# A two-block transformer kernel: residual mix turned by halves in PSUM, attention mask added by VectorE, norm rows fetched earlier, and two expert loads begun by halves

## The reference, cut to what matters

```python
for l in range(2):                       # first block
    mix = conformer_conv(x, ...) if l == 0 else diff_attention(x, ...)
    x = layer_norm(ALPHA * x + mix, ln_mix_g[l], ln_mix_b[l])
    ffn = grouped_moe(x, ...)            # 16 experts of width 512, two for each token
    x = layer_norm(ALPHA * x + ffn, ln_ffn_g[l], ln_ffn_b[l])

h = concat(meta_tokens (16 rows), x)     # second block, 272 rows
xn = rms_norm(h, mix_pre_g)
z, xbc, dt, q, k, v = split(xn @ w_in)
y_ssd = ssd_mixer(z, xbc, dt, ...)       # chunks of 128, the meta rows a chunk of their own
y_sb = rms_norm(stick_breaking_attention(q, k, v), sb_norm_g)
# per head: A[t,s] = sigmoid(z) * prod_{s<j<t}(1 - sigmoid(z)), z = q.k/8, only for s < t
mix = concat([y_ssd, y_sb]) @ w_out
h = h + rms_norm(mix, mix_post_g)
xn = rms_norm(h, ffn_pre_g)
g = causal_dwconv(xn @ w_up[:, :D_FF], conv of 3 taps) # the first token needs two meta rows
f = (gelu(g) * (xn @ w_up[:, D_FF:])) @ w_down
return (h + rms_norm(f, ffn_post_g))[16:]
```

## Time and profile before

| | us |
|---|---|
| median of three runs | 1397.87 (1395.96 to 1400.76) |
| the profiled execution | 1401.46 |
| its span, first to last instruction | 1399.7 |
| PE busy | 1306.0 (93%) |
| DVE busy | 383.9 (27%) |
| ACT busy | 262.6 (19%) |
| POOL busy | 36.0 (3%) |
| moved by DMA | 321.68 MB, mean 230 GB/s |

### The profile page before, as it was taken

How to read it: one execution, slowest core, us unless ns; L and a number is a source line. 1 busy time by engine, 2 the same in 40 slices (tenths; PEclk the granted TensorE clock), 3 DMA queues, 4 the chain that set the end, 5 groups by cost and what they waited for, 6 DMA issues and landing times.

```text
span 1399.7 us, 14987 instructions
## 1 busy us (share of the span) xinstructions
PE 1306.0 (93%) x6166; PEld 815.9 (58%) x6166; DVE 383.9 (27%) x849; ACT 262.6 (19%) x579; POOL 36.0 (3%) x62
## 2 busy tenths in 40 slices
PE   7989899999989998999999799998998979999997
PEld 6754444333437864433433388765775867888743
DVE  0014522111142454312211403455223123222101
ACT  1013311000111343200100321412435012000000
POOL 3110000000000000000000000000000000000000
PEclk9999999999999998999999899899999998999999
DMA  9970899999992063999999923231230162444320
GB/s 307 309 249 2 324 407 428 425 423 429 415 380 86 1 240 147 418 426 424 427 427 427 393 109 121 67 110 43 84 120 1 35 193 73 153 147 161 141 90 30
DMA packets 95087, 321.68 MB, mean 230 GB/s; under 512 B 10099, under 2 KB 47511, under 8 KB 80167
## 3 DMA queue, kind: packets, MB, share of 16 engines
q1 hardware_dynamic: 84368, 301.04, 55.5%
q10 hardware_dynamic: 8662, 12.27, 2.8%
q0 software_dynamic: 1984, 7.34, 1.3%
HBM read 316.30 MB, written 4.34 MB: 229 GB/s over the span
## 4 chain that ended last, share of the span: by engine, by line
PE 87%; DMA 5%; DVE 5%; issue 1%; ACT 1%; DVEq 0%; ACTq 0%; SPq 0%; POOLq 0%
PE psum L255 35%; PE psum L1565 14%; PE psum L1598 7%; PE psum L741 6%; PE psum L2917 5%; DMA ring<-in_moe_w_up 5%; PE psum L1608 4%; PE psum L623 2%; PE psum L909 2%; PE psum L1802 2%; PE psum L531 1%; PE psum L1767 1%; DMA ring<-in_a_w_pw 1%; PE psum L2577 1%; PE psum L1224 1%
## 5 line engine op out<-in xcount | busy, mean ns | idle before, releaser
L255 PE MATMUL psum<-xT,ring 128*128 128x256 f32 (+2 forms) x1792 | 409.7, 390 | 4.6 <-DMA ring<-in_a_w_pw 3.7
L255 PEld LDWEIGHTS psum<-xT,ring 128*128 128x128 f32 x1792 | 344.9, 194 | 65.4 <-issue 10.4
L1565 PE MATMUL psum<-ring,arena 128*64 128x512 f32 x672 | 186.0, 604 | 12.1 <-DMA ring<-in_moe_w_up 6.6
L1565 PEld LDWEIGHTS psum<-ring,arena 128*64 128x64 f32 x672 | 59.8, 139 | 103.1 <-issue 102.8
L1446 DVE TENSOR_TENSOR arena<-psum,arena 64x512 f32<-64x512 f32 x32 | 34.2, 1070 | 215.7 <-ACT arena L1509 215.7
L1598 PE MATMUL psum<-ring,arena 128*64 128x512 f32 x384 | 85.0, 595 | 1.3 <-ACT arena L1526 1.3
L2917 PE MATMUL psum<-ring,arena 128*128 128x512 f32 x176 | 75.7, 592 | 0.0
L1565 PE MATMUL psum<-arena 128*64 128x512 f32 x208 | 70.6, 592 | 0.0
L1509 ACT ACTIVATE arena<-psum 64x512 f32<-64x512 f32 x32 | 18.9, 592 | 269.8 <-PE psum L1565 269.8
L1608 PE MATMUL psum<-arena 128*128 128x512 f32 x128 | 59.5, 605 | 0.0
L2917 PEld LDWEIGHTS psum<-ring,arena 128*128 128x128 f32 x176 | 33.4, 190 | 41.7 <-issue 41.6
(11 more groups left out here) (343 smaller groups left out, 1310.2 us busy)
## 6 DMA issues: line engine op xcount, KB each, us to landing
ring<-in_moe_w_down SPq DMA_DIRECT2D x24, 2048.0 KB, 24.9
ring<-in_moe_w_up SPq DMA_DIRECT2D x22, 2048.0 KB, 20.7
ring<-in_moe_w_gate SPq DMA_DIRECT2D x20, 2048.0 KB, 22.7
ring<-in_w_in SPq DMA_DIRECT2D x11, 2048.0 KB, 22.3
ring<-in_w_up SPq DMA_DIRECT2D x22, 1024.0 KB, 7.7
arena<-in_moe_w_gate SPq DMA_DIRECT2D x6, 2048.0 KB, 26.3
ring<-in_w_down SPq DMA_DIRECT2D x5, 2048.0 KB, 7.8
ring<-in_a_w_pw SPq DMA_DIRECT2D x8, 1024.0 KB, 10.9
```

What stands on the lines that cost most here:

```text
L255: last = nc.tensor.matmul(dst, lhsT, rhs, start=(n == 0), stop=(n == len(pairs) - 1))
L1565: last = pe.matmul(bank(j)[part, :], tokens[:, k, side * SEATS:side * SEATS + SEATS], weights(u + n, k), start=(k == 0), stop=(k == KC - 1))
```

## The change

It has six parts.

1. The rows of the FFN norm of layer 0 are fetched in the conformer stage, behind the last `fetch_shifted`, and those of layer 1 in the attention stage, behind ACT's first four `kq_copy` and a wait for `normed[1]`.
2. The tenth and eleventh unit of each expert layer come by halves (`load_by_halves`): the first halves of both once PE has used slices 0 to 3 of the first `gate_up` (a new semaphore), the second halves when the job is done.
3. One of the 16 q and k products moves from "norm" to chunk 2 of the mixer, ahead of its transposes of xs.
4. The mask is added by DVE (`mask_out`, one operation on both banks), and ACT's `softplus` waits for it. PE's two products go.
5. `project_out`, `mix_post` and `ffn_pre` become `project_out` and `mix_and_turn`. Mix is turned straight into banks 4 to 7 for tiles 1 and 2 (the first half of the width ahead of the last 32 products), the copies to `mix` and the meeting of engines go, ACT and DVE read PSUM, and the tiles go in the order 1, 2, 0.
6. The first four jobs of `ffn` stand as side 1 of c = 0 and 1, then side 0; the first two don't wait until tile 0 of `xT` is copied.

The semaphore of the lambda exponential is replaced by ACT's step semaphore, to make room.

```diff
@@ the loads
+    BY_HALVES = (RING + MORE, RING + MORE + 1)
+        def load_by_halves(layer):
+            first = unit_at[f"moe{layer}"]
+            for half in range(2):
+                if half == 0:
+                    sp.wait_ge(half_used, layer + 1)
+                else:
+                    slot_freed(first + BY_HALVES[0])
+                for u in (first + m for m in BY_HALVES):
+                    kind, _, e = units[u][0]
+                    n = D if kind == "down" else DE
+                    ks = slice(half * 2048 // n, (half + 1) * 2048 // n)
+                    src = a[f"moe_w_{kind}"][layer, e].rearrange("(p k) n -> p k n", p=P)
+                    load(u, src[:, ks, :], slot_k(u, n)[:, ks, :])
...
+                    if (p, side, k) == (0, 0, KC // 2 - 1):
+                        last.then_inc(half_used, 1)
@@ the norm rows
             fetch_shifted(KC - 1)
+            load_norm(1, a["ln_ffn_g"][0], a["ln_ffn_b"][0])
...
+            act.wait_ge(normed[1], 4)
+            load_norm(3, a["ln_ffn_g"][1], a["ln_ffn_b"][1])
             act.preload_act_table_set("natural_log_exp_and_others")
...
     next_norm = {
-        "route0": (1, a["ln_ffn_g"][0], a["ln_ffn_b"][0]), "moe0": (2, a["ln_mix_g"][1], a["ln_mix_b"][1]),
-        "route1": (3, a["ln_ffn_g"][1], a["ln_ffn_b"][1]), "moe1": (4, a["mix_post_g_2"][0]),
+        "moe0": (2, a["ln_mix_g"][1], a["ln_mix_b"][1]), "moe1": (4, a["mix_post_g_2"][0]),
@@ the q and k products
-             ("diag", 2): 2, "norm": 3}
+             ("diag", 2): 2, ("xs", 2): 1, "norm": 2}
@@ the mask
-                first = (BANKS, BANKS + 2, 2)[n % FLIGHT]
-                for side in range(2):
-                    diagonals = psum[:, first + side, :].rearrange("p (a t) -> p a t", a=2)[:, :, 0:P]
-                    last = pe.matmul(diagonals, ident[:, :], not_before[:, :].unsqueeze(1).broadcast_to([P, 2, P]),
-                                     start=False, stop=True, skip_group_check=True)
...
+            def mask_out(n):
+                dve.wait_ge(z_ready, n + 1)
+                first = (BANKS, BANKS + 2, 2)[n % FLIGHT]
+                diagonals = psum[:, first:first + 2, :].rearrange("p s (a t) -> p s a t", a=2)[:, :, :, 0:P]
+                dve.tensor_tensor(diagonals, diagonals, not_before[:, :].unsqueeze(1).unsqueeze(1).broadcast_to([P, 2, 2, P]),
+                                  ALU.add).then_inc(z_masked, 1)
...
+            for n in (2, 3, 4):
+                mask_out(n)
             add_positive(2)
...
                     add_positive(n + 1)
+                if n + 2 < SB_PAIRS:
+                    mask_out(n + 2)
@@ from w_out to the FFN
+            part(0, 0)
+            pe.wait_ge(sb_normed, 1)
+            part(0, 1)
+            part(1, 0)
+            all_read_out(pe, first + 4)
+            for t in (1, 2):
+                turn(0, t)
+            part(1, 1)
+            all_read_out(pe, first + KC)
+            for t in (1, 2):
+                turn(1, t).then_inc(so_summed_mix_turned, 1)
...
+    FFN_ORDER = (1, 2, 0)
...
+            for t in FFN_ORDER:
+                n = TILE_N[t]
+                pe.wait_ge(rms_scaled, base + 4 + count[t])
...
+            for t in FFN_ORDER:
+                mix_squares(t)
+            row_squares(1)
+            row_squares(2)
+            turned_out(1)
+            turned_out(2)
+            row_squares(0)
+            turned_out(0)
...
+            scaled_mix(1)
+            added(1)
+            scaled_mix(2)
+            added(2)
+            scaled_mix(0)
+            scaled_rows(1)
...
+            scaled_rows(2)
+            turned_out(1)
+            turned_out(2)
+            added(0)
+            scaled_rows(0)
+            turned_out(0)
@@ the FFN's jobs
+    UP_ORDER = [(0, 1), (1, 1), (0, 0), (1, 0)] + [(c, side) for c in range(2, FC) for side in range(2)]
+                if j == FJ["up"]:
+                    unit_ready(u)
+                    all_read_out(pe, FJ["ffn_T"] + 4)
+                elif (c, side) == (0, 0):
+                    all_read_out(pe, FJ["up"])
```

More of the change, by code:

```diff
@@ L1741, in turned_heads @@
         return 2 if h < 4 else 3 if h < 6 else 4
+    lam_exp = []
     @stage
@@ L2357, in _ @@
                 n = TILE_N[c]
+                for _ in range(QK_AT.get(("xs", c), 0)):
+                    qk_copy(next(qk_act))
                 if c:
@@ L2841, in _, with part, turn @@
         def _(pe):
[L2843 removed]
+            products(psum[:, BANKS, NEED:L], [(ones[:, :], sqT[:, c, NEED:L]) for c in range(KC)]).then_inc(so_summed_mix_turned, 1)
             w = unit_at["w_out"]
[L2846 to L2847 removed]
+            first, parts = FJ["w_out"], ((w, yT), (w + 1, sbT))
+            def part(half, i):
+                u, lhs = parts[i][0] + 2 * half, parts[i][1]
+                unit_ready(u)
+                for c in range(4 * half, 4 * half + 4):
+                    if i == 0:
+                        take_bank(first + c)
+                    for k in range(KC):
+                        last = pe.matmul(bank(first + c)[:, NEED:L], slot_k(u)[:, k, (c % 4) * P:(c % 4) * P + P],
+                                         lhs[:, k, NEED:L], start=(i == 0 and k == 0), stop=(i == 1 and k == KC - 1))
+                    if i == 1:
+                        last.then_inc(job_done, 1)
+            def turn(half, t):
+                for c in range(4):
+                    last = pe.transpose(psum[:, BANKS + 2 * (t - 1) + half, c * P:c * P + P],
+                                        mixT[:, 4 * half + c, TILE_AT[t]:TILE_AT[t] + P], ident[:, :])
+                return last
+            part(0, 0)
[9 more added lines that the diff above has]
+                turn(1, t).then_inc(so_summed_mix_turned, 1)
+            for half in range(2):
+                j = first + KC + half
+                take_bank(j)
+                for c in range(4):
+                    last = pe.transpose(bank(j)[0:META, c * P:c * P + P], mixT[:, 4 * (1 - half) + c, 0:META], ident[:, :])
+                last.then_inc(job_done, 1)
         @block.scalar
@@ L2865, in _ @@
         @block.vector
         def _(dve):
-            j = FJ["w_out"] + KC
-            for half in range(2):
-                for t in ALL:
-                    n = TILE_N[t]
-                    job_ready(dve, j)
-                    dve.tensor_copy(mix[0:n, t, half * 512:half * 512 + 512], bank(j)[0:n, :]).then_inc(
-                        bank_free[j % BANKS], 1)
-                    j += 1
-    @stage
-    def mix_post():
-        post_norm(4, "mix_post", ALL, lambda t: mix[:, t, :], lambda t: mix_n[:, t, :], mix_added)
```

149 lines of the change are left out of this document (116 added, 33 removed).

## The result

| | before | changed |
|---|---|---|
| median, us | 1397.99 (1395.96 to 1400.76, 4 runs) | 1388.08 (1386.20 to 1390.34, 4 runs) |
| ratio | | 0.9926, 95% interval 0.9907 to 0.9946 |
| profiled execution, us | 1401.46 | 1389.67 |
| span, us | 1399.7 | 1388.0 |
| PE busy, us | 1306.0 | 1296.9 |

The change saves 9.9 us by the medians. Timed again later beside 29 runs of before, it came to 1387.04 and 0.9914 (0.9900 to 0.9928), which is 12.0 us. The forecast was 14.0: the direction and the range (1378.5 to 1390.0) hold, the sum is 2 to 4 us too large. The two profiled executions lie 11.8 apart, as near as the medians, so the traces can be read for where the rest went.

The account below looks back on a forecast made before the run. The prediction took PE to bound the kernel (87% of the span by the chain of work). Its terms, -1.7 - 1.9 + 0.4 - 3.7 - 2.1 - 5.0 + 0 = -14.0, took the median 1397.87 to 1383.9 us, range 1378.5 to 1390.0.

Parts of the forecast that it names:

- Experts, layer 0: Layer 0's expert weight loads: early norm rows and halves shorten PE's waits by 1.7 us; bounds 0 to -3.9.
- Experts, layer 1: Layer 1's expert weight loads: the same lead shortens PE's waits by 1.9 us; bounds 0 to -3.9.
- theory A: Expectation for after2: if layer 1's lag was one execution's accident, PE's wait there is 1.3 to 1.8 us shorter.
- rival B: Expectation for after2: layer 1's lag belongs to the changed order of loads and recurs; PE's wait stays at 2.8 us.
- The price of halves: Expert weight loads: two more transfers a layer cost 0; at the other end, four more would add 12.4 us.
- Rival (e): Weight loads: the 3.1 us of a load that are no bytes are paid one behind the other, 1396.3 us; chance 0.02.
- The mask: Attention: moving the mask from PE to DVE saves 2.1 us for pairs 0 and 1, 5.0 for pairs 2 to 7.
- The ring: Attention loop of logits, mask, three ACT steps, addition, values: masks of pairs 5, 6 and 7 give back 2.8 us.
- rival (d): Attention: DVE's addition that writes PSUM is dear, kernel slower than before; 1403.7 us at 4.0 a mask; chance 0.03.
- From w_out to the FFN: Last product of w_out to first of the FFN: 20.3 us against 20.1, so 0; bounds -4 and +3.
- rival (b): The stretch from w_out to the FFN goes to its bounds: 1379.9 us (chance 0.10) or 1386.9 (0.08).
- Rival (a): Expert layers: their part is worth nothing, as later units issued on PE's jobs take the lead back; 1387.5 us; chance 0.12.

Follow-up runs that it names:

- late_warm: late plus 14 products of 128x256 that nobody reads, in PE's wait ahead of the transposes of the normed rows; 1379.63 us, 0.9875 of before.
- mask_split: The changed kernel with the masks of pairs 5, 6 and 7 back on PE, those of 0 to 4 on DVE; 0.9929 of before.
- after2: The changed kernel timed once more, with nothing altered; 1387.04 us, 0.9914 of before.
- late: The changed kernel with PE's transposes of tile 0 (16 rows) moved behind the FFN's first two jobs; 1383.71 us, 0.9895 of before.

## Why the prediction was right, and where it was off

- **Experts, layer 0: forecast -1.7, measured -1.6** (207.3 to 205.7 in the first pair of profiles; of the other executions with halves seven have 205.1 to 205.8 and one 207.4, and the five without have 206.6 to 207.9). By the means of nine executions with halves and five without it is -1.9. The bound by 8.0 us for a load into an empty queue was right: 7.8 to 8.4 in eight executions, 8.8 in the one with 207.4. The sentence that neither part alone would do it was wrong: the halves alone do.
- **Experts, layer 1: forecast -1.9, measured -0.2 there.** This is the step that failed. It was carried over from layer 0 by the one row of 9.9, and the window of layer 1 was not read; it shows 428 GB/s and no hole. What the bytes of part 1 gave moved the first increment of the fourteenth unit by 1.4 and the last, for which PE waits, by about half of that on average. Two executions with both parts (late_warm, mask_split) do show it: 206.5 and 206.4 in layer 1 against 207.4 to 207.8 without. So the gain is 0 to 1.4, and 0.5 by the means of nine executions with halves and five without. The lag of the last increment is no accident of one execution, as theory A of after2 had it: it came in all seven executions with both parts and in none of the others, which is rival B, with the addition that it can fall into layer 0 instead. Why the two parts together bring it stays open.
- **The price of halves: forecast 0, right.** The four halves landed 2.5 apart in layer 0 and layer 1. Rival (e) is dead: two more transfers a layer cost nothing that shows. The Trainium skill, page "DMA: Bandwidth & Descriptors", section "Anatomy of one DMA", gives the fit that the prediction quotes under the path of GpSimd; these loads are issued by SP. By it a 2 MB load into an empty queue would take 6.8 us (an estimate by that page), and 7.8 to 8.3 were measured; that the fixed part overlaps agrees with the 2.5 between landings.
- **Norm rows elsewhere: forecast +0.4, measured +0.3.** From the last expert product of layer 0 to the first scores of the attention it is 67.5 to 67.6 without part 1 and 67.7 to 67.9 with it, leaving out executions in which a stretch at the lower clock adds 0.9 to either.
- **The q and k product: forecast -3.7, by rows right** (11.16 to 7.50 in the norm, the gap of 2.84 filled, 0.3 of the next gap left). The stretch moved by 3.1 in the first pair and by 3.7 in the means of six executions without the move and eight with it.
- **The mask: forecast -7.1, measured 7.1 alone and -9.1 in the first pair.** Like with like it is 7.9 or 6.3, by the clock, and 7.5 by the means of six executions each. PE was to be spared 9.9, which counts two masks at the lower clock (2.00 and 1.53), and was spared 8.9. The ring was to cost 2.8, and PE's waits rose by 1.0 where a window reads 0.79 and by 2.6 in late, where none does; in the first case mask_split shows that the 1.0 isn't due to the loop's masks. So both terms were too large, and as they are of opposite sign the sum is good, in part by luck. The 0.70 for an operation that writes PSUM put rival (d) away. The 7.1 of the kernel with part 4 alone goes with the clock: PE's waits for DVE there are 5.8 and a window reads 0.75.
- **From w_out to the FFN: forecast 0, measured +0.3 in the stretch and, by the means, +1.9 behind it.** The 19.5 of the stretch was forecast as 19.4, and the 0.9 ahead of it is there. Left out was the clock at which the FFN starts (0.65 to 0.72 over its first 8 us). With layer 1 this is the other term that was mis-sized, and the larger one; the upper bound of rival (b), +3, was nearly reached, though behind the stretch and not in it.

Together, by the means over all profiles: -1.9, -0.5, +0.3, -3.7, -7.5 and +2.2 make -11.1, between the two timings (9.9 and 12.0). A possible price of part 1 in the conformer stage is not in it. The parts timed alone add up to more: 2.4 for the experts, 7.1, 5.9 and -1.3 make 14.1, but each has an interval of about 2 us to either side. Rival (a), the experts worth nothing, was half the truth.

## What to carry to other kernels

A term read at one of two equal-looking layers must be read at the other too: a window over the same place would have shown that layer 1 has no hole. Look at what stands ahead in an engine's list before rebuilding what feeds it: the 16 rows of tile 0 held up 256 others, and moving their eight transposes behind two jobs took 4.4 us off a stretch whose whole re-staging had changed it by 0.3. And a wait can cost more than its own length: products that nobody reads, put into a wait of 7.9 us, did not shorten that wait, but the stretch became 1.4 us shorter by what ran behind it.

## What the hardware showed unexpectedly

- An fp32 addition of 128x512 that reads and writes PSUM takes 0.70 us on DVE, the same as reading alone (0.69).
- In late the granted clock fell while PE stood idle for 7.9 us (0.81 over the idle time, 0.56 over the transposes that followed); in late_warm, where products that nobody reads fill 6.3 us of it, it stayed at 1.00. The same 16 transposes took 3.67 and 1.96 us.
- The same code takes different times by where the lower clock falls: over six kernels with the attention of before it takes 84.4 (granted clock 1.00), 86.0 to 86.1 (one 8 us window at 0.79) or 87.3 to 87.5 (that window at 0.60 to 0.62), and the stretch from the FFN to the end 235.3 or 235.4 (1.00 over its first 8 us) or 236.9 to 237.0 (0.79 to 0.80). Differences of single profiles under 3 us say little without the clock beside them.
- The 16 increments of one 2 MB load came over 0.8 to 5.3 us while the stream ran at about 426 GB/s, and a reader waits for the last.
